# One PSUM bank, one copy and one turn for the conditioning vectors of a two-block network

## The reference, cut to what matters

```python
def adaln(c, w_ada, b_ada):                  # w_ada: 1024 x 3072 for each of two layers
    shift, scale, gate = split(silu(c) @ w_ada + b_ada, 3)
for layer in range(2):
    shift, scale, gate = adaln(c, w_ada[layer], b_ada[layer])
    c_shift, c_scale, c_gate = adaln(c_ctx, w_ada[layer], b_ada[layer])
```

## Time and profile before

| | us |
|---|---|
| median of 3 runs | 2292.65 (2289.89 to 2295.39) |
| the profiled execution, its own time | 2293.27 |
| its span | 2291.5 |
| PE busy / weight loads busy | 2200.4 / 1427.9 |
| DVE busy | 1266.7 |
| ACT busy | 696.5 |
| HBM read | 528.91 MB, 231 GB/s over the span |

### The profile page before, as it was taken

How to read it: one execution, slowest core, us unless ns; L and a number is a source line. 1 busy time by engine, 2 the same in 40 slices (tenths; PEclk the granted TensorE clock), 3 DMA queues, 4 the chain that set the end, 5 groups by cost and what they waited for, 6 DMA issues and landing times. The chain is left out here.

```text
span 2291.5 us, 41474 instructions
## 1 busy us (share of the span) xinstructions
PE 2200.4 (96%) x17257; PEld 1427.9 (62%) x17263; DVE 1266.7 (55%) x2570; ACT 696.5 (30%) x904; POOL 13.1 (1%) x25
## 2 busy tenths in 40 slices
PE   7999999999899899999999999999999999898988
PEld 7899899999899733333333333333336784677856
DVE  5765534437865345444544444444468665847783
ACT  6464533337464200010001000100024222634452
POOL 0000000000000000000000000000001000000000
PEclk9999999999999799999999999999999999999999
DMA  6244566655334299999999999999991120016400
GB/s 260 105 147 148 206 254 250 265 188 218 110 132 146 94 373 408 388 377 376 408 393 363 386 402 384 379 386 400 386 379 37 74 93 36 1 56 133 109 17 19
DMA packets 81812, 532.05 MB, mean 232 GB/s; under 512 B 16935, under 2 KB 17224, under 8 KB 17480
## 3 DMA queue, kind: packets, MB, share of 16 engines
q1 hardware_dynamic: 81528, 528.95, 60.7%
q10 hardware_dynamic: 144, 1.05, 0.1%
HBM read 528.91 MB, written 1.05 MB: 231 GB/s over the span
## 5 line engine op out<-in xcount | busy, mean ns | idle before, releaser
L512 PE MATMUL ps<-ring,arena 128*32 128x512 f32 (+1 forms) x3056 | 894.6, 566 | 3.9 <-DMA ring<-panels 2.7
L512 PE MATMUL ps<-ring,hT 128*32 128x512 f32 x5376 | 795.8, 593 | 0.0
L512 PEld LDWEIGHTS ps<-ring,arena 128*32 128x32 f32 x3056 | 231.5, 110 | 596.5 <-issue 545.0
L1432 ACT ACTIVATE arena<-ps 96x256 f32<-96x256 f32 (+3 forms) x210 | 100.3, 485 | 882.0 <-PE ps L512 860.2
L2452 DVE STREAM_TRANSPOSE arena<-arena 32x64 f32<-32x64 f32 x1344 | 316.2, 235 | 20.8
L2499 DVE SCALAR_TENSOR_TENSOR arena<-arena,rt,ps 96x256 f32<-96x256 f32 x112 | 53.4, 477 | 475.1 <-ACT arena L1432 475.1
L512 PEld LDWEIGHTS ps<-ring,hT 128*32 128x32 f32 x5376 | 212.9, 110 | 7.3 <-issue 7.3
L512 PE MATMUL ps<-h_parts,ring_low 128*128 128x256 f32 x704 | 199.9, 284 | 0.0
L512 PE MATMUL ps<-h_parts,B_high 128*128 128x256 f32 x1024 | 189.1, 287 | 1.8 <-DVE h_parts L2058 1.2
L512 PE MATMUL ps<-y_parts,ring_low 128*128 128x256 f32 (+1 forms) x512 | 173.3, 339 | 0.0
L2314 DVE TENSOR_TENSOR W_low<-ring,W_high 128x2048 fp32r<-128x2048 f32 x42 | 96.2, 2292 | 128.1 <-ACT W_high L1432 128.1
(11 more groups left out here) (281 smaller groups left out, 3401.8 us busy)
## 6 DMA issues: line engine op xcount, KB each, us to landing
ring<-panels SPq DMA_DIRECT2D x496, 1024.0 KB, 7.4
arena<-rpb SPq DMA_DIRECT2D x32, 64.0 KB, 8.5
cst<-consts SPq DMA_DIRECT2D x1, 1632.0 KB, 11.9
xT<-x SPq DMA_DIRECT2D x1, 1024.0 KB, 5.0
cT<-ctx SPq DMA_DIRECT2D x1, 1024.0 KB, 11.0
arena<-dft SPq DMA_DIRECT2D x1, 1024.0 KB, 17.3
y<-xT ACTq DMA_DIRECT2D x1, 1024.0 KB, 3.9
proj<-w SPq DMA_DIRECT2D x1, 512.0 KB, 9.4
```

The source lines that it names most:

```text
L512: return nc.tensor.matmul(o, w, m, start=start, stop=stop, skip_group_check=skip)
L1432: return nc.scalar.activation(o, i, fn, **kw)
```

## The change

All twelve sets accumulate in bank 2. `cond_wide` becomes eight blocks of 64 columns, with the two vectors at columns 30 and 31 of each; `condition_at(j, k)` takes the 32 columns that begin at 30 - 2j, so that set j lands in the rows 2j and 2j + 1 of each group of 32 and adds zeros to the other rows. Bank 2 is cleared once at the head of the dense layer, and every matmul of `conditioning` accumulates. One copy on ACT and four matmuls on PE, with 24 moving columns each, take the place of twelve copies and 48 matmuls with two columns. They stand where the last set's copy and turn stood. The waits between the copies, the turns and the cond panels go. `conditioned` reads bank 3 in another order.

```diff
-        def ada_rows(j):
-            return arena[:, 8704 + (j % 2) * 512:9216 + (j % 2) * 512]
-        def ada_bank(j):
-            return 1 if j == ADA - 1 else 2
-        cond_wide = arena[:, 8192:8448]
-        cond_pick = arena[:, 8448:8480]
+        ada_rows = arena[:, 8704:9216]
+        ADA_BANK = 2
+        COND_AT = 30
+        cond_wide = arena[:, 8192:8704].rearrange("p (k n) -> p k n", k=KD)
+        cond_pick = arena[:, 9216:9248]
+        def condition_at(j, k):
+            return cond_wide[:, k, COND_AT - 2 * j:COND_AT - 2 * j + 32]
...
-                        last = mm(bank(ada_bank(n // 2))[g:g + 32, (n % 2) * S:(n % 2 + 1) * S],
-                                  cond_wide[:, 32 * k:32 * k + 32], slot(p, k * S, (k + 1) * S), k < 4, k >= 4)
+                        last = mm(bank(ADA_BANK)[g:g + 32, (n % 2) * S:(n % 2 + 1) * S],
+                                  condition_at(n // 2, k), slot(p, k * S, (k + 1) * S), False, True, True)
...
-                def conditioning_turn(j):
-                    pe.wait_ge(sem("ada_rows_copied"), j + 1)
+                def conditioning_turn():
+                    pe.wait_ge(sem("ada_rows_copied"), 1)
                     for c in range(4):
-                        last = mm(bank(3)[:, (4 * j + c) * 2:(4 * j + c) * 2 + 2], ada_rows(j)[:, c * P:(c + 1) * P],
-                                  cond_pick[:, 0:2], True, True)
+                        last = mm(bank(3)[:, c * 2 * ADA:(c + 1) * 2 * ADA], ada_rows[:, c * P:(c + 1) * P],
+                                  cond_pick[:, 0:2 * ADA], True, True)
...
                 def last_conds():
-                    pe.wait_ge(sem("ada_rows_copied"), ADA - 2)
...
-                def last_turns():
-                    conditioning_turn(ADA - 2)
-                    conditioning_turn(ADA - 1)
                 zero(0)
+                zero(ADA_BANK)
...
-                        elif 2 <= n < ADA:
-                            conditioning_turn(n - 2)
...
-                        elif n % 2 == 0:
-                            pe.wait_ge(sem("ada_rows_copied"), n // 2)
                         conditioning(p0 + i, n)
...
                 if layer:
-                    act.wait_ge(DONE, p0 - 2)
-                    conditioning_rows(ADA - 2)
                     act.wait_ge(DONE, p0)
-                    conditioning_rows(ADA - 1)
+                    conditioning_rows()
...
-            def conditioning_rows(j):
-                if j >= 2:
-                    act.wait_ge(sem("ada_turned"), j - 1)
-                f(ada_rows(j), bank(ada_bank(j)), ACT.Copy).then_inc(sem("ada_rows_copied"), 1)
+            def conditioning_rows():
+                f(ada_rows, bank(ADA_BANK), ACT.Copy).then_inc(sem("ada_rows_copied"), 1)
...
-                    elif kind == "cond" and n % 2:
-                        act.wait_ge(DONE, p0 + i + 1)
-                        conditioning_rows(n // 2)
...
                 step(V.memset(cond_wide, 0.0))
-                V.tensor_copy(cond_wide.rearrange("p (k n) -> p k n", k=KD)[:, :, 0:2],
+                V.tensor_copy(cond_wide[:, :, COND_AT:COND_AT + 2],
                               cond[:, :].rearrange("p (k s) -> p k s", s=2))
...
-                dve.wait_ge(sem("ada_turned"), ADA)
+                dve.wait_ge(sem("ada_turned"), 1)
+                turned = bank(3)[:, 0:8 * ADA].rearrange("p (c j s) -> p j c s", c=4, s=2)
```

More of the change, by code:

```diff
@@ L894, in dense_layer @@
                         down(q, n)
-                return last_conds, last_turns
+                return last_conds, conditioning_turn
             def router():
@@ L1102, in _ @@
                     last_conds()
-                    project1(layer, last_turns)
+                    project1(layer, last_turn)
                 mix_out(layer)
                 if layer == 0:
-                    last_conds, last_turns = dense_layer(at[0])
+                    last_conds, last_turn = dense_layer(at[0])
                     at[0] += len(DENSE)
@@ L2355, in conditioned @@
             def conditioned():
-                dve.wait_ge(sem("ada_turned"), ADA)
+                dve.wait_ge(sem("ada_turned"), 1)
+                turned = bank(3)[:, 0:8 * ADA].rearrange("p (c j s) -> p j c s", c=4, s=2)
                 for layer in range(2):
-                    v = bank(3)[:, 48 * layer:48 * layer + 48].rearrange("p (c s) -> p c s", s=2)
-                    o = ada(layer, 0, 48).rearrange("p (c s) -> p c s", s=2)
+                    v = turned[:, ADA // 2 * layer:ADA // 2 * (layer + 1), :, :]
+                    o = ada(layer, 0, 48).rearrange("p (j c s) -> p j c s", c=4, s=2)
                     step(V.tensor_tensor(o, v, sml[:, S_ADA + 24 * layer:S_ADA + 24 * layer + 24]
-                                         .unsqueeze(2).to_broadcast([P, 24, 2]), ALU.add))
+                                         .rearrange("p (j c) -> p j c", c=4).unsqueeze(3)
+                                         .to_broadcast([P, ADA // 2, 4, 2]), ALU.add))
             dve.wait_ge(sem("x_landed"), 16)
```

## The result

The changed kernel took 2277.6 us (2276.45 to 2282.04, 6 runs) where the kernel before took 2292.77 us in the same set (6 runs): ratio 0.9944, 95% interval 0.993 to 0.9957, 15.2 us faster. The forecast was 8.5 us and 2284.1, with a range that began at 2280.5, so the direction was right and the size was not. The profiled execution of the changed kernel has a span of 2275.0 us.

What follows compares the result with a forecast made beforehand. PE was taken to bound the dense layer. Ten turns (8.1 us) plus the last turns (0.4) gave 8.5 us, taking the median from 2292.65 to 2284.1; own range 2280.5 to 2287.5, for 8 in 10 2280.5 to 2288.5.

Steps and rivals of the forecast that it cites:

- Ten turns in the dense layer: PE between up and down panels: removing ten turns saves 0.81 us each, 8.1 us, the main term.
- Cover on the other engines: Dense layer: gate-panel splits have 8.5 us of slack against 0.8 us removed per period, and loads have room; nothing becomes late.
- The last turns: Layer 1's projection: one turn fewer would give 0.9 us, but the second panel's DVE split limits the gain to 0.4 us.
- the two bounds: The one new turn with 24 moving columns: eight records take between 0.81 us (two columns) and 1.0 us (128 columns).
- Cond panels: Dense layer, 24 panels: accumulating and reading 64-column weight blocks at an offset costs nothing; removed waits also give nothing.
- the new zero: Head of dense layer: one more bf16 matmul, hidden by PE's 1.93 us wait for DVE; uncovered at most 0.5 us, once.
- DVE, ACT: Clearing `cond_wide` doubles from 0.27 us within idle time; ACT loses eleven copies, 6.5 us in all; neither changes the time.
- The second rival: Cond panels: accumulation breaks the four column groups' overlap, 1.7 us more per panel, 41 us, 2325 (or 2305); chance 0.02.
- The gain carried through: Stages after the dense layer start on events, not fixed times, so the whole 8.5 us reaches the end.
- the first rival: Lower-clock stretches from 700 to 800 us: gain partly given back, 8.5 shrinking to 4.5 us, 2288.1; chance 0.09.
- The three widths: Forecast's own range: some 2 us for medians of few runs, 1.5 for the clock, 0.4 for the last turns.
- The span behind 540 us changed by more than 2 us: Sign, behind the dense layer: such a change in either direction would prove the prediction as a whole wrong.

Runs made afterwards that it cites:

- the ten idle turns: Changed kernel with ten sets of four unused two-column matmuls put back between up and down panels, without copies and waits; 2291.9 us, kernel before beside it 2291.5.
- the row of forty: Changed kernel with five idle turns (forty records) in a row behind the one real turn in layer 1's projection, also called five late turns; 2287.6 us.
- four sets: Kernel before and unaltered changed kernel measured side by side four times; ratios 0.9944, 0.9963, 0.9959 and 0.9955.

## Why the prediction was right or wrong

**Ten turns in the dense layer (8.1 us).** The mechanism was right, the term was mis-sized by a tenth: 0.89 us each, 8.9 in all. The error is in where the step was read. The matmul behind a turn starts 0.81 us late, and the one behind that by another 0.08 us: in the rows of the ten idle turns 289.02 and 289.22 are 0.20 us apart, not 0.12. The step of 0.112 us a record in the row of forty gives the same 0.89 for eight.

**Cover on the other engines.** Right. PE is busy 262.81 of 264 us in the dense layer with the copies gone and 262.83 with them put back.

**The last turns (0.4 us).** Right in size and in cause: 0.48 us, with PE released by the split on DVE. From the first record of the one turn with 24 columns to the next group it is 0.81 us (525.11 to 525.92, in the kernel with five late turns), the lower of the two bounds; the 0.97 in the rows is a length to the end of the last record, 0.95 with two columns.

**Cond panels, the new zero, DVE, ACT (nothing).** Right: 24.9 us of cond panels in both, a wait of 1.72 us left behind the zero. The second rival, four column groups that lose their overlap, is refuted by the same row.

**What was not in the sum.** The norm ahead of layer 1 was 0.4 to 0.5 us shorter in the first pair of traces (a load landed 9.29 us into ACT's wait and not 9.75). The prediction put nothing there. The kernels with turns in the dense layer take 6.0 to 8.7 us for it, those without 5.8 to 6.0.

**The gain carried through, and the first rival.** The sum for the part that belongs to the change would have been 8.9 + 0.4 = 9.3 us, 2283.3, or some 10.2 us with the estimated 0.9 of the norm; three of four sets (9.1, 9.9, 11.6) lie around these two. The step that failed is "it is carried through" with 1.5 us for the clock and nothing for any other stage behind 540 us. In the first pair of traces the stretch behind the last turn was 6.7 us shorter, and it takes 1743.3 to 1748.5 us in three traces of the kernel before and 1741.8 to 1746.3 in four of the changed one. The prediction named the right stretches and priced a bad fall of the lower clock at 4 us, but gave the good fall only 1.5 us in its range, with the words that the stretch could as well shrink. (The three widths 2, 1.5 and 0.4 us add up to 2280.2 to 2288.0 and not to the 2280.5 to 2287.5 that it states; that decides nothing.) The traces show that stage alone 30.3 to 34.1 us long for the same work, the second network 543.4 to 545.6, and the experts, at the full clock, 857.0 to 860.3. With the same 4 us on the lower side the range would have begun at 2278, and with the second network's 2 us at 2276. What made the six runs of the first set lie 3 to 5 us below the later ones stays open; the three later sets, with 10.2 us in the mean, are the better measure of the change. "The span behind 540 us changed by more than 2 us" came true in the first pair of traces, and the repeated traces of either kernel show that no change of the program is needed for that.

## What to carry to other kernels

A small matmul on a PE that never waits did not get cheaper with fewer moving columns: four of them with two columns were 0.89 us, and records with 24 and with two columns followed each other at the same 0.11 us. Merging twelve such groups into one by letting zeros be added elsewhere in the bank cost nothing in the accumulation. Price an inserted piece from the last instruction ahead of it to the second one behind it, and compare with a place where the same neighbours meet. Where PE's granted clock is below 1 in the trace, put an equal price on both sides of the forecast for how that stretch may fall in another execution, allow for the spread of long stages too, and take more than one trace and one set of runs before a difference there is given to the change.

## What the runs showed of the hardware

- PE that is busy all the time with matmuls of two moving columns can be granted the lower clock: 0.73 over 525 to 550 us with 88 such records in a row, 0.93 with 40, 1.00 with none; 5.4 us were paid for 4.1 us of them, and 15.6 for 9.4.
- With zeros multiplied in bf16 during PE's waits (31 matmuls of 512 columns in all) the medians were 3.2 and 3.3 us lower of 2282, with the mean granted clock of the runs up by 0.002 to 0.004; the traces do not show in which stage.
- The 0.89 us of a turn (eight records) hardly changed between ten spread over the dense layer with copies and waits (8.9 us of dense layer) and ten without them (8.7). A matmul that adds to a bank cost the same as one that overwrites it: half of the cond panels' matmuls overwrote before, all add now, and 384 records take 24.9 us in both kernels.
- One program repeats its dense layer to 0.1 us from trace to trace and its second network to 2 us, the latter in step with the time that PE spent at the lower clock level in it (10.2, 13.7 or 17.1 us).
